# Two blocks on one core: the fourth merge gate's products move into the levels of the RWKV chains

## The reference

```
h = rmsnorm(x);  p = h @ w_in          # p is split into all the parts below
o_a = mla_branch(...)                  # latent attention, 8 heads
o_b = fox_branch(...)                  # attention with forget gates, 8 heads
o_c = rwkv_branch(...)                 # RWKV-7: a recurrence over tokens, 8 heads of 64
g_a, g_b, g_c = split(merge_cols, 3)   # each 256 x 1024
merged = sigmoid(g_a) * (o_a @ w_pa) + sigmoid(g_b) * (o_b @ w_pb) + sigmoid(g_c) * (o_c @ w_pc)
x = x + merged @ w_out
```

## Time and profile before

| | us |
|---|---|
| median of 3 runs | 1445.94 (1445.26 to 1446.96) |
| the profiled execution | 1446.18 |
| its span | 1444.0 |
| TensorE busy | 1384.2 (96%) |
| VectorE busy | 801.3 (55%) |
| ScalarE busy | 564.5 (39%) |

### The profile page before, as it was taken

The page is one execution under the profiler, slowest core; times in us unless marked ns, Lnnn a source line. Parts: engine busy times, 40 slices in busy tenths (PEclk is TensorE's granted clock), DMA queues, the critical chain, the costliest instruction groups (busy, mean ns, idle before and its releaser), DMA issues.

```text
span 1444.0 us, 24636 instructions
## 1 busy us (share of the span) xinstructions
PE 1384.2 (96%) x10704; PEld 1009.3 (70%) x10704; DVE 801.3 (55%) x1186; ACT 564.5 (39%) x842; POOL 52.5 (4%) x43
## 2 busy tenths in 40 slices
PE   6999999999899999999899999999999999999998
PEld 6887445444596544544499787788779978777886
DVE  4666121121557212212569887677666988768764
ACT  4552101111443111111346658643454665864342
POOL 0010000000120000000000000010000000001000
PEclk9999999999999999999999999999999999999999
DMA  9438999999367999999344344320364443432032
GB/s 385 156 142 337 423 422 421 423 421 422 154 243 309 379 421 422 423 421 423 150 167 153 140 146 149 143 90 4 117 214 164 150 153 133 164 128 103 4 118 88
DMA packets 47490, 340.26 MB, mean 236 GB/s; under 512 B 5296, under 2 KB 5296, under 8 KB 7568
## 3 DMA queue, kind: packets, MB, share of 16 engines
q1 hardware_dynamic: 45504, 328.03, 57.5%
q0 software_dynamic: 1872, 10.57, 2.0%
HBM read 337.53 MB, written 1.05 MB: 234 GB/s over the span
## 4 chain that ended last, share of the span: by engine, by line
PE 82%; DVE 9%; ACT 6%; issue 2%; DMA 0%; DVEq 0%; SPq 0%; ACTq 0%
PE bank L547 48%; PE bank L910 15%; PE bank L951 8%; PE bank L854 4%; PE bank L553 2%; DVE d_lo L1876 2%; ACT d_hi L1460 2%; PE bank L883 1%; ACT arena L1421 1%; PE bank L888 1%; ACT arena L1646 1%; DVE arena L2393 1%; PE bank L893 1%; PE bank L936 0%; DMA ring<-wfirst 0%
## 5 line engine op out<-in xcount | busy, mean ns | idle before, releaser
L1876 DVE TENSOR_TENSOR d_lo<-ring,d_hi 128x2048 fp32r<-128x2048 f32 (+2 forms) x111 | 249.4, 2256 | 106.0 <-ACT d_hi L1460 105.7
L1460 ACT ACTIVATE d_hi<-ring 128x2048 fp32r<-128x2048 f32 (+2 forms) x115 | 216.2, 1887 | 138.0 <-PE bank L547 113.2
L547 PE MATMUL bank<-arena 64*64 64x64 f32 (+7 forms) x3680 | 165.3, 235 | 15.8 <-issue 6.0
L547 PE MATMUL bank<-xT_hi,d_hi 128*128 128x256 f32 x592 | 168.4, 284 | 4.6 <-ACT arena L1421 3.4
L547 PEld LDWEIGHTS bank<-arena 64*64 64x64 f32 (+4 forms) x3680 | 143.2, 139 | 35.4 <-issue 15.3
L547 PE MATMUL bank<-xT_hi,d_lo 128*128 128x256 f32 x592 | 166.9, 282 | 0.0
L547 PE MATMUL bank<-xT_lo,d_hi 128*128 128x256 f32 x592 | 166.5, 281 | 0.0
L1421 ACT ACTIVATE arena<-bank 128x512 f32<-128x512 f32 (+4 forms) x188 | 100.2, 551 | 166.1 <-PE bank L547 133.2
L547 PE MATMUL bank<-d_hi,xT_hi 128*128 128x512 f32 (+1 forms) x400 | 158.5, 396 | 3.6 <-DVE d_lo L1876 3.3
L547 PE MATMUL bank<-d_hi,xT_lo 128*128 128x512 f32 (+1 forms) x400 | 156.9, 392 | 0.0
L547 PE MATMUL bank<-d_lo,xT_hi 128*128 128x512 f32 (+1 forms) x400 | 156.0, 390 | 0.0
(11 more groups left out here) (357 smaller groups left out, 2030.8 us busy)
## 6 DMA issues: line engine op xcount, KB each, us to landing
ring<-wmoe SPq DMA_DIRECT2D x84, 1024.0 KB, 16.6
ring<-wsecond SPq DMA_DIRECT2D x80, 1024.0 KB, 4.6
arena<-wmoe SPq DMA_DIRECT2D x72, 1024.0 KB, 16.9
ring<-wfirst SPq DMA_DIRECT2D x30, 1024.0 KB, 4.8
wide<-wmoe SPq DMA_DIRECT2D x24, 1024.0 KB, 19.7
xT_raw<-wmoe SPq DMA_DIRECT2D x12, 1024.0 KB, 19.8
rows<-lnrows POOLq DMA_DIRECT2D x4, 1024.0 KB, 7.7
ring<-wsecond SPq DMA_DIRECT2D x4, 848.0 KB, 10.4
```

The source lines that it names most:

```text
L547: mark(nc.tensor.matmul(o, lhsT, rhs, start=start, stop=stop, skip_group_check=loose), full)
L1460: nc.scalar.activation(high_of(u)[:, 0:width], raw[u % NRAW][:, 0:width], ACT.Copy).then_inc(sem("piece_high"), 1)
L1876: v.tensor_tensor(d_lo[u % NRAW][:, 0:width], raw[u % NRAW][:, 0:width], high_of(u)[:, 0:width], SUB).then_inc(sem("piece_low"), 1)
```

## The change

In both layers the 48 matmuls of mg4 leave their place after the chains. `gate_step(tt, at)` makes the group `at` of tile tt, in bank 7. Two groups stand in each of the four levels of a tile: one ahead of level_t(0), one behind level_t(1) and ahead of level_x(0). The first result is complete in the fourth level of tile 0; ScalarE copies it unchanged to sgm after the level copies, once add_merged has run, and later makes the sigmoid in place. The second stays in bank 7 until `merge_sigmoid`. sgm2 is given up, sgm takes its place. VectorE's `gate_ready` waits for the sigmoid in place as well.

```diff
@@ tensor
+                gate_w = []
+                def gate_step(tt, at):
+                    part, k, tok = at // 4, at % 4, slice(tt * P, (tt + 1) * P)
+                    if at == 0:
+                        pe_eng.wait_ge(bank_free[7], pe.reuse(7))
+                    if tt == 0 and k == 0:
+                        gate_w.append([v3(half, 4) for half in piece(f"mg4.{l}", part, part > 0)])
+                    elif tt and at == 4:
+                        pe.close(1)
+                    hi, lo = gate_w[part]
+                    three(banks[7][:, :], (xT[0][:, at, tok], xT[1][:, at, tok]), (hi[:, k, :], lo[:, k, :]),
+                          at == 0, at == KD - 1, full=7 if at == KD - 1 else None)
+                    if at == KD - 1:
+                        pe.note(f"mg4.{l}.{tt}", 7)
...
                     turned_rows("Kp", lw[tt], 7)
+                    kp_used = pe.used(7)
                     for lev in range(1, LEVELS - 1):
+                        gate_step(tt, 2 * lev - 2)
                         level_t(0, False)
                         level_t(1, False)
+                        gate_step(tt, 2 * lev - 1)
                         for par in range(2):
...
-                    pe_eng.wait_ge(bank_free[7], pe.used(7))
+                    pe_eng.wait_ge(bank_free[7], kp_used)
...
-                merge_gates(f"mg4.{l}", (7, 6))
                 merge_gates(f"mg5.{l}", (5, 6))
@@ scalar
+                        if not normed and n == 0 and tt == 0:
+                            nc.scalar.activation(o, o, ACT.Sigmoid).then_inc(act_step, act.sends(act_step))
+                            MADE[names[n]] = act.sent[act_step.name]
...
                         copy_out(TTm[:, par, :, :], 5 + par, v3(banks[5 + par][:, 4 * CH:8 * CH], 4))
+                    if tt == 0:
+                        act_eng.wait_ge(sem("sums_added"), l + 1)
+                        copy_out(sgm[:, 0, 0:512], 7, banks[7][:, :])
                     copy_out(WU[:, 1, :, :], 6, v3(banks[6][:, :], 4))
...
-                merge_sigmoid(sgm2, None, f"mg4.{l}", f"mg5.{l}")
+                merge_sigmoid(sgm, None, f"mg4.{l}", f"mg5.{l}")
@@ vector
                 dve_eng.wait_ge(bank_free[b], free)
+                if tt == 0 and name in MADE:
+                    dve_eng.wait_ge(act_step, MADE[name])
...
-                v.tensor_tensor(merged, merged, s, ADD).then_inc(dve_step, dve.sends(dve_step))
+                v.tensor_tensor(merged, merged, s, ADD).then_inc(sem("sums_added"), dve.sends(sem("sums_added")))
...
-                merge_last(sgm2, f"mg4.{l}", f"mg5.{l}")
+                merge_last(sgm, f"mg4.{l}", f"mg5.{l}")
```

More of the change, by code:

```diff
@@ L343, in two_blocks @@
         assert cl.at <= FREE_A
-        sgm2 = v3(arena[:, PCOL_END:PCOL_END + 2 * D], TT)
         cl = Carve(FREE_B)
@@ L428, in two_blocks @@
         BANK_USE = {}
+        MADE = {}
         class TensorCounts(Counts):
@@ L1668, in merge_sigmoid @@
                         o = s[:, tt, n * 512:(n + 1) * 512]
-                        if b < 5:
+                        if not normed and n == 0 and tt == 0:
+                            nc.scalar.activation(o, o, ACT.Sigmoid).then_inc(act_step, act.sends(act_step))
+                            MADE[names[n]] = act.sent[act_step.name]
+                        elif b < 5:
                             act_eng.wait_ge(bank_full[b], full)
```

## The result

The kernel after takes 1469.55 us (median of 4 runs, 1468.43 to 1470.77), the one before, in the same comparison, 1446.31 (4 runs, 1445.26 to 1446.96). The ratio is 1.0163, with a 95% interval of 1.0147 to 1.0179: slower by 23.2 us. 1467.3 was predicted.

The account below looks back on a forecast made before the run. TensorE's issue and waits were taken to bound the kernel. Chains +26.8, tails -9.4 and clock +4.0 gave +21.4 on the profiled 1446.18, 1467.6, or 1467.3 us for the median; range 1458 to 1472.5.

Parts of the forecast that it names:

- The bound: Whole kernel: TensorE is busy for 96% of the span, so only its issue and its waits count.
- The group, 1.01: Levels: a moved group of three products costs 1.01 us with two changes of array shape, against 0.70 in place.
- Rival 3: Levels: changes of shape cost nothing, a group is 0.70 us; +12.0, 1457.9 us; chance 8%.
- The wait for Kp's copy: First group of each tile waits for ScalarE's copy of Kp; level_t(0) starts 1.68 (tile 0) or 1.69 us late.
- The waits hidden: Levels: groups hide 2.47 us of waits in tile 0, 1.64 in tile 1; net +6.3 and +7.1.
- Rival 5: Levels: groups go wholly into waits, so only the tail counts; 1440.5 us; chance 4%.
- The edits at no cost: ScalarE's bank 7 copy, the sigmoid in place, counters and SyncE's earlier load add nothing; uncovered, the copy costs 0.6 a layer.
- The tail: After the chain TensorE idles 6.5 us for VectorE's split of mg5's weights; 4.7 saved a layer, not 11.2.
- Rival 4: Tail: no wait appears, as mg5's low half is ready when the chain ends; +4.4, 1450.3 us; chance 4%.
- The clock: Over mg5: the 6.5 us idle brings the granted clock to 0.50, losing 2.0 us a layer, +4.0.
- rival 1: Tail: the clock doesn't fall; +17.4, 1463.3 us; chance 12%.
- rival 2: Tail: the low clock lasts longer over work, 3.4 us a layer; +24.2, 1470.1 us; chance 8%.

Follow-up runs that it names:

- experiments 1 and 3: Kernel before, mg4 kept, with its 16 groups repeated unread in the levels: 1473.76 us; the same with 12 64x64 matmuls replacing each group: 1464.05 us.
- experiments 7 to 9: Kernel after with a level's two groups together ahead of level_x(0): 1462.17 us; plus mg5's weights split early: 1447.50; then groups only at waits: 1444.00.
- experiment 2: Kernel before, mg4 kept, with 24 unread 64x64 matmuls (48 instructions) for each group added in the levels: 1488.21 us.
- Experiment 4: Kernel after, with mg5's first piece of weights split in the levels of tile 1 and its second ahead of gn_scale: 1452.96 us.
- experiment 6: Kernel after, with 7 unread float32 products a layer filling TensorE's idle ahead of mg5: 1466.09 us.
- experiments 7, 11 and 12: Kernel after, level's groups paired: 1462.17 us; early split, groups at waits between level_x(0) and level_x(1), more in tile 1: 1440.66; early split, pairs there: 1444.17.

## Why the prediction was right, and where its sizes were off

**The bound.** That only TensorE's issue and its waits count is borne out by the sum: the three segments make 22.7 of 23.7 us.

**The group, 1.01.** Right, from two sides: start to start in the trace after, and 0.3 for the changes of shape by experiments 1 and 3. Rival 3, 0.70 a group and 1457.9, is out. The bounds of 0.70 and 1.01 were real ones: the change of shape never seen before, from 128x512 to 64x64, measured 0.32. Its stand-in in the trace before had given 0.33, and the sum had 0.32 without saying why; the slip is 0.01.

**The wait for Kp's copy.** Right: 998.32 + 0.89 is the start of level_t(0), with an idle of 0.74 ahead of the group in both layers.

**The waits hidden.** The waits for ScalarE went as forecast, but I took it that what a group hides is gone for good. In tile 1 it isn't: +7.4 instead of +7.1. (Rival 5, groups wholly in waits, is out with a level of 4.88.) Behind the fourth level, where no group follows level_x(1), the starts of two single matmuls, 1019.085 and 1019.362, are 0.28 apart; before, the same two had 0.07. In the kernel after such a gap stands once a tile, since in the other levels the next group covers it. Where no group stands ahead of the next level_t(0) (experiments 7 to 9) it stands behind every group or pair but that of the first level, which has other work behind it, and there it makes up much of the missing gain. The other 0.1 is four levels of 4.88 instead of 4.85.

In tile 0 the term of 6.3 is met in layer 2. In layer 1 it is 5.7, because the trace before holds an idle there that its second layer and the trace after don't have, and the profile shows nothing that ended it:

```profile
980.82 1.73 PE L547 MATMUL bank<-arena 64*64 64x64 f32 x52 [0.75 <-issue]
```

So "the second layer's rows repeat the pattern" was not quite so; the baseline of layer 1 was 0.6 too long. Of the other traces only that of experiment 2 has this idle, 0.75 long too and at the same matmul; what it is stays open.

**The edits at no cost.** Nothing in the trace after speaks against them: no row of TensorE names ScalarE's copy of bank 7, the sigmoid in place or a load.

**The tail.** The wait stands where it was put, ended by what was named (VectorE's low half, queued behind `gn_mean` and `gn_square`), 6.41 long against 6.5 in start-to-start time that includes 0.07 of modelled overlap. Rival 4 is out. Experiment 4 tests that this wait is what separates -4.7 from -11.2: with the split made earlier, the tail falls to 12.2.

**The clock.** Its fall was right and rival 1 is out; the size was low. 2.0 a layer had been taken, and 13.74 - 11.2 = 2.5 was lost, a little more than the bound of 2.4; the filling in experiment 6 gave back 2.5. The low stretch reached from 1031.57 to 1041.81, so 5.45 us of it lay on work, more than the 4.9 behind the idle of 3.96, and there 13 products stood for 23. Twice 0.5 is the largest miss in the sum. It lies on the way to rival 2 (3.4), which allowed for it.

**Sum.** The span grew by 23.7, and +21.4 was forecast. The chains gave 5.7 + 6.3 + 7.4 + 7.4 = 26.8, as forecast, but only because the 0.6 too much in tile 1 and the 0.6 too little in layer 1's tile 0 cancel, which is luck. The tails gave -4.1 instead of -5.4, 1.0 of the 1.3 between them the clock. The last 1.0 is the chance difference ahead of the first chain.

## What to carry to other kernels

Before work is moved into waits, count the waits in the timeline one by one: 1.6 us a tile in the levels can't hold 5.6 us of products, and work that leaves its place may have been the cover of another engine there; move that engine's work first. Where two units of the moved work have the array's other shape, put them side by side, but don't count on the saved changes alone: in a level they gave 0.06 us, since 0.25 came back as a wait. Put them at the step where both producers, the one that is waited for now and the one that will be next, gain by it: the same pair of groups cost 1.58 us a level ahead of level_x(0) and 1.30 one step later.

## What the runs showed of the hardware

**Changes of shape.** From 64x64 to 128x512 products and back costs 0.31 us a round trip by the rows and 0.30 to 0.35 by the runs, in three places: 0.12 before the first full product, 0.11 behind it, 0.09 on the way back. The 0.11 isn't the shape's own: behind a wait between products of one shape (experiment 4, 1037.37 and 1037.71) the second one is 0.34 later too, instead of 0.23. The Trainium skill, "TensorEngine Tiling (Array Packing)", section Key Properties, says that TensorE is drained there; the runs agree, and the size is theirs.

**The clock doesn't fall at every idle of a length.** Ahead of the router's products (L547, 128x512, about 709) all traces have an idle of 3.4 us. Before, the granted clock fell behind it; in the kernel after it didn't. A window of 3.0 us there, first in the kernel before, then after:

```profile
708.40:711.40 3.00, 3.00 (x5) 1.32 (x6) 2.93 (x8) 1.44 (x4) 0.00 (x0) 0.66 0.02 5
```

```profile
709.20:712.20 3.00, 3.00 (x7) 1.33 (x8) 2.93 (x8) 1.44 (x4) 0.00 (x0) 1.00 0.02 5
```

The code is the same. Here the fall costs nothing that can be seen: from the end of this idle to that of the one at 894 TensorE takes 185.5 us before and 185.7 after. There (L547, 128x256; 2.6 us in every trace) it does cost. In eleven of the fourteen traces the clock fell behind it, in those of experiments 7, 11 and 12 it didn't. The last of these, to be held against 15 products in the same 3.30 us before:

```profile
893.90 0.36 PE L547 MATMUL bank<-xT_hi,d_hi 128*128 128x256 f32 x1 [2.62 <-ACT arena L1441]
...
893.90:897.20 3.30, 3.30 (x28) 3.30 (x29) 3.23 (x5) 3.17 (x3) 0.00 (x0) 1.00 0.60 196
```

From the end of that idle to the mark of the first chain these three take 61.7 us, all others 63.0 to 63.3, and their marks are the three earliest (955.65 to 955.85, the others 957.0 to 959.2). So one fall of the clock was worth 1.5 us there. What decides whether it comes isn't shown, since the code up to there is the same. It is probably part of what single executions of a kernel here differ by, but not of the 1.0 us between before and after, which both had it. Behind the idle of 6.41 it fell in both layers, for 10.24 us in both.

**Matmuls of float32.** A product of 64 x 64, and one of 128 x 128 by 128 x 512, with float32 operands appear as two instructions each (0.03 and 0.43 us of issue each), one with the rounded type as one. Two of my experiments missed by that.
